# Reordering the attention steps of three engines around four weight products per head

## The chip, the cores and the metric

The kernel runs on one core of a Trainium2 chip. The metric is the device time of one execution in microseconds (us), the median of several runs. Five engines of the core work side by side, each through its own list of instructions in order: TensorE (PE in the profile: matrix products and transposes into the PSUM banks), VectorE (DVE), ScalarE (ACT), GpSimd (POOL, here mainly the issuer of small transfers) and SyncE (SP, which issues the weight transfers). They wait for each other through counting semaphores.

## What is computed

The reference runs two transformer blocks over 256 tokens of width 2048. The first has two layers (neighbourhood, dilated and memory attention); the second has a state-space mixer, differential attention and a gated feed-forward part. The change lies in the differential attention of the second block. Cut to that:

```python
q = rms_norm_2(q, q_norm_w) * 64 ** -0.5        # 8 heads, each with two maps of width 64
k = rms_norm_2(k, k_norm_w)
s = einsum('bqhmd,bkhmd->bhmqk', q, k) + bias   # masked by chunks of 64
p = softmax(s)
p = p[:, :, 0] - lam * p[:, :, 1]
o = einsum('bhqk,bkhe->bqhe', p, v)
o = rms_norm_2(o, subln_w) * (1 - lambda_init)
```

with `q`, `k`, `v` and the state-space input `u` of each head from `h @ w_in`.

## The kernel before

Activations are kept feature-major: 128 features on the partitions, 256 tokens along the row. The weights stream through a ring of four slots of 128x1024 (`w_raw`). Each fp32 chunk is split into two parts: ACT rounds it into `w_hi` (`split_hi`, L717), DVE subtracts into `w_lo` (`split_lo`, L1297), and SP refills the slot when DVE is done with it. PE multiplies each chunk by three products of 8 tiles (L1991 to L1993). Two chunks, 48 products, make one job: 128 output features for all tokens. `split_hi(p, c)` may write a slot only when PE has used up the chunk four places earlier (`w_free`).

The eight heads take one period each, `head_2(i)`, with four jobs (q, k, v, u). While head i is projected, head i-1 goes through scores and softmax (`prev`), and head i-2 through the product with v and the output norm (`prev2`). So every engine carries three heads' steps, written by hand between the jobs:

- PE: job 0, `values2` (probabilities by v), job 1, `scores2` (two transposes and eight score products), `output_sums` (the sum of squares for the output norm, L2180), jobs 2 and 3, `turn2` (transposes of the probabilities, L2203), `norm_sums` (L2211).
- DVE: `split_lo(p, 1)`, u out of PSUM, `attn_0` (q and k norm), `split_lo(p, 2)`, `attn_1` (clamp and square of the output, L1591 and L1593), q out of PSUM, `split_lo(p, 3)`, `attn_2` (bias added and row maxima, L1599 to L1603; mean, `osq` and reciprocal for the output norm, L1607 to L1611), k out of PSUM, `attn_3` (the two softmax maps combined, L1618 to L1627), `split_lo(p, 4)`, v out of PSUM, `attn_4` (output norm applied, L1635 and L1637).
- ACT: `attn_0` (L949, L952), `split_hi(p, 1)`, `attn_1` (Ln, Exp for the q and k norm, L957 and L959; output out of PSUM), `split_hi(p, 2)`, `split_hi(p, 3)`, `attn_2` (v out of PSUM, L976; four Exp, L982; Sqrt, L987), `split_hi(p, 4)`, `attn_3` (squares of q and k, L992).

The third chunk pair of a period is chunks 4 and 5; `split_lo(p, 4)` and `split_hi(p, 4)` already prepare chunks 0 and 1 of the period after. Head 1 has no `prev2` part. The last heads' steps run in the first two of the eight periods of gate products that follow, `gates(p, j, attn=...)`, where the state-space mixer's sections and a Sigmoid per job (`gate_out`, L1029) lie between the same steps. A function of ACT from another table than the last one gets an ACT_TABLE_LOAD ahead of it; the compiler puts it there. Small tensors of this part all lie in one buffer, so the profile names them `arena` or `cols`.

The semaphores that matter: `osq_clamped` (L1593 done) lets PE start `output_sums`; `osum_done` lets DVE start L1607; `ov_step` (L1611 done) lets ACT take the Sqrt; `scores2_done`, `max2_ready` and `exp2_done` lead from the scores over the maxima to the Exps and on to L1618; `probs2_ready` (L1627 done) lets PE start `turn2`.

Of the kernel before, what the change touches and what calls it, by code (L numbers as in the profile page):

```python
# [10 lines left out]
ALU = mybir.AluOpType  # L11
ACT = mybir.ActivationFunctionType
AX_X = mybir.AxisListType.X

P = 128
# [35 lines left out]
SUBLN_EPS = 1e-5  # L51
# [13 lines left out]
FLT_MAX = 3.4028234e38  # L65
SUB_SCALE = 2.0 ** -12
# [3 lines left out]
def build(nc, ap, out):  # L70
    ctx = ExitStack()
    with ctx:
# [253 lines left out]
        osum_done = sem("osum_done")  # L326
# [369 lines left out]
        def _(act):  # L696
# [273 lines left out]
                act.dma_start(u_d[i - 1], zz).then_inc(u_stored, 16)  # L970

            def attn_2(i, prev, prev2):
                if prev:

                    act.wait_ge(scores2_done, i)
                    act.activation(v2_tok, v_ps[:, 0, :].rearrange("p (a b) -> p a b", a=NQ),  # L976
                                   ACT.Copy).then_inc(v2_ready, 1)
                    act.wait_ge(max2_ready, i)
                    for m in range(2):
                        for t in range(NQ):  # L980
                            k = NQ * m + t
                            e = act.activation(sc[m][:, t, :], sc[m][:, t, :], ACT.Exp, bias=neg_max2[:, k:k + 1],  # L982
                                               accum_out=row_sum2[:, k:k + 1])
                    e.then_inc(exp2_done, 1)
                if prev2:
                    act.wait_ge(ov_step, 2 * (i - 1))
                    act.activation(o_root, ov, ACT.Sqrt).then_inc(o_root_ready, 1)  # L987

            def attn_3(p, i):

# [200 lines left out]
        def _(dve):  # L1191
# [401 lines left out]
                    dve.tensor_tensor(osq, osq, osq, ALU.mult).then_inc(osq_clamped, 1)  # L1593

            def attn_2(i, prev, prev2):
                if prev:
                    dve.wait_ge(scores2_done, i)
                    dve.wait_ge(bias2_in, 64 * i)
                    dve.tensor_tensor(sc[0], s_ps[:], bias2, ALU.add)  # L1599
                    dve.tensor_tensor(sc[1], o_ps[:], bias2, ALU.add).then_inc(biased2, 1)  # L1600
                    dve.wait_ge(biased2, i)
                    dve.tensor_reduce(neg_max2[:, 0:2], sc[0], AX_X, ALU.max, negate=True)
                    dve.tensor_reduce(neg_max2[:, 2:4], sc[1], AX_X, ALU.max, negate=True).then_inc(max2_ready, 1)  # L1603
                if prev2:
                    dve.wait_ge(osum_done, i - 1)

                    dve.tensor_scalar(osq, p_ps[:, 0, :], FLT_MAX * SUB_SCALE ** 2, SUB_SCALE, ALU.is_lt, ALU.mult)  # L1607
                    dve.tensor_scalar(ov, p_ps[:, 0, :], 1.0 / P, SUBLN_EPS * SUB_SCALE ** 2,
                                      ALU.mult, ALU.add).then_inc(ov_step, 1)
                    dve.wait_ge(ov_step, 2 * (i - 2) + 1)  # L1610
                    dve.reciprocal(ov, ov).then_inc(ov_step, 1)  # L1611

            def attn_3(i, prev):
                if prev:

                    h = i - 1
                    dve.wait_ge(exp2_done, i)
                    dve.reciprocal(coef2, row_sum2).then_inc(comb_step, 1)  # L1618
                    dve.wait_ge(comb_step, 3 * h + 1)
                    dve.tensor_scalar(coef2[:, 2:4], coef2[:, 2:4], neg_lam, None, ALU.mult).then_inc(comb_step, 1)  # L1620
                    dve.wait_ge(comb_step, 3 * h + 2)
                    for t in range(NQ):
                        e = dve.tensor_scalar(sc[0][:, t, :], sc[0][:, t, :], coef2[:, t:t + 1], None, ALU.mult)
                    e.then_inc(comb_step, 1)
                    dve.wait_ge(comb_step, 3 * h + 3)
                    for t in range(NQ):
                        e = dve.scalar_tensor_tensor(out=sc[0][:, t, :], in0=sc[1][:, t, :],  # L1627
                                                     scalar=coef2[:, 2 + t:3 + t], in1=sc[0][:, t, :],
                                                     op0=ALU.mult, op1=ALU.add)
                    e.then_inc(probs2_ready, 1)  # L1630

            def attn_4(i, prev2):
                if prev2:
                    dve.wait_ge(o_root_ready, i - 1)
                    dve.tensor_tensor(o_root, o_root, osq, ALU.mult).then_inc(om_step, 1)  # L1635
                    dve.wait_ge(om_step, i - 1)
                    dve.scalar_tensor_tensor(out=ov, in0=o_sb, scalar=vecs[:, 2:3], in1=o_root,  # L1637
                                             op0=ALU.mult, op1=ALU.mult).then_inc(yo_ready, 1)

            def head_2(i, prev=True, prev2=True, prev3=True):  # L1640
                p = P_QKV + i
                split_lo(p, 1)
                if prev:
                    if prev2:
                        dve.wait_ge(u_stored, 16 * (i - 1))
                    evac_u(p - 1)
                    dve.wait_ge(z_free, taken(p - 1, 3))
                    dve.sem_inc(u_ready, 1)
                attn_0(i, prev, prev3)
                split_lo(p, 2)  # L1650
                attn_1(i, prev, prev2)
                evac2(qk[:, 0, :], p, 0, 4)
                split_lo(p, 3)
                attn_2(i, prev, prev2)
                evac2(qk[:, 1, :], p, 1, 4)
                attn_3(i, prev)
                split_lo(p, 4)
                if prev:
                    dve.wait_ge(scores2_done, i)
                evac2(v2_t, p, 2, 4)  # L1660
                attn_4(i, prev2)

# [121 lines left out]
            def gates(p, j, first=False, attn=None):  # L1786
                split_lo(p, 1)
                if not first:
                    evac_gate(p - 1, 3, 4 * j - 1)
                if attn is not None:  # L1790
                    attn_0(attn[0], attn[1], attn[3])
                section(4 * j)
                split_lo(p, 2)
                evac_gate(p, 0, 4 * j, first)
                if attn is not None:
                    attn_1(*attn[:3])
                section(4 * j + 1)
                split_lo(p, 3)
                evac_gate(p, 1, 4 * j + 1)
                if attn is not None:  # L1800
                    attn_2(*attn[:3])
                section(4 * j + 2)
                split_lo(p, 4)
                evac_gate(p, 2, 4 * j + 2)
                if attn is not None:
                    attn_3(*attn[:2])
                    attn_4(attn[0], attn[2])
                section(4 * j + 3)


# [168 lines left out]
        def _(pe):  # L1979
# [234 lines left out]
            def head_2(i, prev=True, prev2=True, sums=False):  # L2214
                p = P_QKV + i
                job2(p, 0, x_hi, x_lo, (lambda kt: pe.wait_ge(x_lo_ready, DEPTH * KT + kt + 1)) if sums else None, 4)
                if sums:
                    pe.wait_ge(sq_summed, summed(DEPTH, 0) - 1)
                    pe.matmul(p_ps[:, 0, :], ones[:], sq_sum[:, 0, :], start=True, stop=True)
                    column_sums(p_ps[:, 1, :], sq_sum[:, 1, :], sums_ready)  # L2220
                if prev2:
                    values2(i)
                job2(p, 1, x_hi, x_lo, ring=4)
                if prev:
                    scores2(i, prev2)
                if prev2:
                    output_sums(i)
                job2(p, 2, x_hi, x_lo, ring=4)
                job2(p, 3, x_hi, x_lo, ring=4)
                pe.wait_ge(qk_sq_ready, i + 1)  # L2230
                if prev:
                    turn2(i, prev2)
                norm_sums(i)
# [37 lines left out]
            def gates(p, j, first=False, attn=None):  # L2271
                for c in range(4):
                    job2(p, c, x_hi, x_lo)
                    if attn is not None:
                        i, prev = attn
                        if c == 0:
                            values2(i)
                        if c == 1:
                            if prev:
                                scores2(i, True)  # L2280
                            output_sums(i)
                        if c == 3 and prev:
                            turn2(i, True)
                    for n in range(PAIRS):
                        if FRONT[n] == 4 * j + c:
                            inputs(n)
                        if FRONT[n] + 2 == 4 * j + c:
                            outputs(n)
# [249 lines left out]
```

## Time and profile before

| | |
|---|---|
| median of three runs | 2573.4 us (2573.39 to 2573.99) |
| the profiled execution | 2573.4 us, span 2571.7 us |
| PE busy | 2473.0 us, 96% of the span |
| DVE busy | 1695.0 us, 66% |
| ACT busy | 1214.3 us, 47% |
| POOL busy | 629.8 us, 24% |
| chain that ended last | PE 74%, DVE 12%, issue 5%, ACT 4%, POOL 3% |
| HBM traffic | 189 GB/s over the span |

The time is what the host's runs report; the span is that of the profiled execution's instructions, and 1.7 us lie around it. Matmuls are pipelined: a row of 0.28 us starts every 0.12 us at full clock, so PE's progress is read from start to start and not from the busy column. PE is busy nearly throughout; what is left are waits of one engine for another inside the stages. The eight head periods lie from 1136 to 1358 us, and the two gate periods that still carry attention steps from 1358 to about 1426 us.

### The profile page before, as it was taken

The page shows a single profiled execution, that of the slowest core. Times are in us where ns is not written, and L with a number is a line of the kernel's source. Part 1 is how long each engine was busy: PE and PEld are TensorE (multiplying, and loading weights), DVE is VectorE, ACT ScalarE, POOL GpSimd, SP SyncE. Part 2 cuts the span into 40 slices and gives each one's busy share as a digit, 9 for nine tenths or more (in the row PEclk, how much of TensorE's full clock was granted, in tenths as well). Part 3 has the DMA queues.
Part 4 walks back from the last instruction along what each step waited for, and adds up shares of the span by engine and source line. Part 5 has one row for each costly group of instructions (what it writes and reads, how often), then busy time and mean ns, then how long its engine had stood idle before and what let it go on. Part 6 is the DMA issues. An engine that isn't in the chain of part 4 may idle for free.

```text
span 2571.7 us, 50514 instructions
## 1 busy us (share of the span) xinstructions
PE 2473.0 (96%) x18072; PEld 2348.5 (91%) x18072; DVE 1695.0 (66%) x2556; ACT 1214.3 (47%) x1813; POOL 629.8 (24%) x1047
## 2 busy tenths in 40 slices
PE   7899999989999999999998999999999999999999
PEld 7899999889899999899998999999888888888888
DVE  7877676557777777668887776665555555555555
ACT  5345444445555555555655334434544444444443
POOL 3300031248778887120010231001000000000000
PEclk9999999999999999999999999999999999999999
DMA  6655576555555555456465676665766777667664
GB/s 234 196 189 189 182 212 195 173 174 169 169 178 180 183 192 186 153 164 207 160 194 163 214 253 229 197 218 168 194 191 187 186 189 187 188 185 185 186 187 156
DMA packets 217449, 484.85 MB, mean 189 GB/s; under 512 B 22760, under 2 KB 120724, under 8 KB 217088
## 3 DMA queue, kind: packets, MB, share of 16 engines
q1 hardware_dynamic: 182912, 415.29, 53.2%
q0 software_dynamic: 13216, 37.93, 4.9%
q10 hardware_dynamic: 21216, 30.22, 3.6%
q8 instruction: 67, 1.10, 0.2%
q14 instruction: 38, 0.31, 0.0%
HBM read 455.00 MB, written 31.08 MB: 189 GB/s over the span
## 4 chain that ended last, share of the span: by engine, by line
PE 74%; DVE 12%; issue 5%; ACT 4%; POOL 3%; ACTq 1%; DMA 1%; DVEq 0%; POOLq 0%; SPq 0%
PE z_ps L1991 14%; PE z_ps L1992 13%; PE z_ps L1993 13%; PE z_ps L2328 6%; PE z_ps L2327 6%; PE z_ps L2333 6%; DVE w_lo L1297 4%; ACT w_hi L717 2%; POOL arena L559 1%; PE v_ps L2361 1%; PE o_ps L2362 1%; PE o_ps L2361 1%; PE p_ps L2361 1%; PE p_ps L2360 1%; PE o_ps L2360 1%
## 5 line engine op out<-in xcount | busy, mean ns | idle before, releaser
L1297 DVE TENSOR_TENSOR w_lo<-w_raw,w_hi 128x1024 fp32r<-128x1024 f32 x520 | 638.5, 1256 | 316.3 <-ACT w_hi L717 313.7
L1991 PE MATMUL z_ps<-x_hi,w_hi 128*128 128x256 f32 x2816 | 823.8, 293 | 17.3 <-DVE w_lo L1290 14.2
L1992 PE MATMUL z_ps<-x_lo,w_hi 128*128 128x256 f32 x2816 | 806.9, 287 | 0.0
L1993 PE MATMUL z_ps<-x_hi,w_lo 128*128 128x256 f32 x2816 | 806.5, 286 | 0.0
L717 ACT ACTIVATE w_hi<-w_raw 128x1024 fp32r<-128x1024 f32 x520 | 532.8, 1051 | 264.4 <-PE z_ps L1993 213.4
L1991 PEld LDWEIGHTS z_ps<-x_hi,w_hi 128*128 128x128 f32 x2816 | 550.1, 195 | 24.3 <-issue 16.5
L1992 PEld LDWEIGHTS z_ps<-x_lo,w_hi 128*128 128x128 f32 x2816 | 550.3, 195 | 1.2
L1993 PEld LDWEIGHTS z_ps<-x_hi,w_lo 128*128 128x128 f32 x2816 | 550.1, 195 | 0.0
L1881 DVE TENSOR_TENSOR w_lo<-w_raw,w_hi 128x1024 fp32r<-128x1024 f32 x262 | 320.8, 1226 | 314.8 <-ACT w_hi L1141 314.8
L1141 ACT ACTIVATE w_hi<-w_raw 128x1024 fp32r<-128x1024 f32 x262 | 277.7, 1060 | 427.9 <-PE z_ps L2333 272.8
L2327 PE MATMUL z_ps<-w_hi,x_hi 128*128 128x512 f32 x704 | 275.2, 391 | 0.6 <-DVE res L1857 0.6
L2328 PE MATMUL z_ps<-w_hi,x_lo 128*128 128x512 f32 x704 | 274.4, 390 | 0.0
L1991 PE MATMUL z_ps<-y_hi,w_hi 128*128 128x256 f32 x768 | 220.7, 287 | 14.2 <-DVE y_lo L1344 10.6
L1992 PE MATMUL z_ps<-y_lo,w_hi 128*128 128x256 f32 x768 | 219.0, 285 | 0.0
L1993 PE MATMUL z_ps<-y_hi,w_lo 128*128 128x256 f32 x768 | 218.9, 285 | 0.0
L2333 PE MATMUL z_ps<-w_lo,x_hi 128*128 128x512 f32 x704 | 188.3, 389 | 0.0
L1991 PE MATMUL z_ps<-m_hi,w_hi 128*128 128x256 f32 x576 | 166.6, 289 | 3.9 <-DVE m_lo L1853 2.6
L1991 PEld LDWEIGHTS z_ps<-y_hi,w_hi 128*128 128x128 f32 x768 | 149.0, 194 | 22.0 <-issue 21.9
L1992 PE MATMUL z_ps<-m_lo,w_hi 128*128 128x256 f32 x576 | 163.6, 284 | 0.0
L1993 PE MATMUL z_ps<-m_hi,w_lo 128*128 128x256 f32 x576 | 163.6, 284 | 0.0
L2327 PEld LDWEIGHTS z_ps<-w_hi,x_hi 128*128 128x128 f32 x704 | 132.3, 188 | 27.6 <-DVE res L1857 0.8
L2333 PEld LDWEIGHTS z_ps<-w_lo,x_hi 128*128 128x128 f32 x704 | 132.2, 188 | 27.5
(382 smaller groups left out, 4123.2 us busy)
## 6 DMA issues: line engine op xcount, KB each, us to landing
w_raw<-in_w SPq DMA_DIRECT2D x704, 512.0 KB, 4.2
w_raw<-in_w SPq DMA_DIRECT2D x80, 384.0 KB, 4.9
res<-tab_d POOLq DMA_DIRECT2D x32, 384.0 KB, 4.6
w_raw<-in_w SPq DMA_DIRECT2D x80, 128.0 KB, 2.9
tab_d<-arena ACTq DMA_DIRECT2D x32, 256.0 KB, 2.1
tab_d<-arena POOLq DMA_DIRECT2D x32, 128.0 KB, 3.5
sg_d<-arena ACTq DMA_DIRECT2D x32, 128.0 KB, 4.4
arena<-sg_d POOLq DMA_DIRECT2D x16, 256.0 KB, 3.7
```

The lines of the kernel that those rows point to most:

```text
L717: act.activation(w_hi[:, n % RING, :], w_raw[:, n % RING, :], ACT.Copy).then_inc(w_hi_ready, 1)
L1141: act.activation(w_hi[:, k % RING, :], w_raw[:, k % RING, :], ACT.Copy).then_inc(w_hi_ready, 1)
L1297: dve.tensor_tensor(w_lo[:, n % RING, :], w_raw[:, n % RING, :], w_hi[:, n % RING, :].bitcast(F32), ALU.subtract).then_inc(w_lo_ready, 1)
L1881: dve.tensor_tensor(w_lo[:, k % RING, :], w_raw[:, k % RING, :], w_hi[:, k % RING, :].bitcast(F32), ALU.subtract).then_inc(w_lo_ready, 1)
L1991: pe.matmul(z, wh, hi[:, kt, :], start=(first and i == 0), stop=False)
L1992: pe.matmul(z, wh, lo[:, kt, :], start=False, stop=False)
L1993: m = pe.matmul(z, wl, hi[:, kt, :], start=False, stop=(last and i == len(kts) - 1))
L2327: pe.matmul(z[t], x_hi[:, kt, r], hi_w[:, :, i * P:(i + 1) * P], start=(kt == 0), stop=False)
L2328: pe.matmul(z[t], x_lo[:, kt, r], hi_w[:, :, i * P:(i + 1) * P], start=False, stop=False)
L2333: m = pe.matmul(z[t], x_hi[:, kt, t * P:(t + 1) * P], lo_w[:, :, i * P:(i + 1) * P], start=False, stop=(kt == KT - 1))
L2360: pe.matmul(z, wh, y_hi[:, at + kt, :], start=(kt == 0), stop=False)
L2361: pe.matmul(z, wh, y_lo[:, at + kt, :], start=False, stop=False)
```

## The change

The order of the same instructions is changed on three engines; none is added or dropped in the source.

- PE: `output_sums(i)` now comes ahead of `scores2(i)`, in the heads and in the gate periods.
- DVE: in `attn_2` the output-norm part (L1607 to L1611, with its wait for `osum_done`) comes ahead of bias and maxima. In the head periods the combination of the maps (`attn_3`) moves from ahead of `split_lo(p, 4)` to behind it and behind v's way out of PSUM; `attn_4` is joined to it. In the gate periods `attn_3` and `attn_4` keep their place.
- ACT: in `attn_2` the Sqrt, with its wait for `ov_step`, comes ahead of v's copy and the four Exps.

```diff
--- before.py
+++ after.py
@@ -970,6 +970,9 @@
                 act.dma_start(u_d[i - 1], zz).then_inc(u_stored, 16)
 
             def attn_2(i, prev, prev2):
+                if prev2:
+                    act.wait_ge(ov_step, 2 * (i - 1))
+                    act.activation(o_root, ov, ACT.Sqrt).then_inc(o_root_ready, 1)
                 if prev:
 
                     act.wait_ge(scores2_done, i)
@@ -982,9 +985,6 @@
                             e = act.activation(sc[m][:, t, :], sc[m][:, t, :], ACT.Exp, bias=neg_max2[:, k:k + 1],
                                                accum_out=row_sum2[:, k:k + 1])
                     e.then_inc(exp2_done, 1)
-                if prev2:
-                    act.wait_ge(ov_step, 2 * (i - 1))
-                    act.activation(o_root, ov, ACT.Sqrt).then_inc(o_root_ready, 1)
 
             def attn_3(p, i):
 
@@ -1593,6 +1593,14 @@
                     dve.tensor_tensor(osq, osq, osq, ALU.mult).then_inc(osq_clamped, 1)
 
             def attn_2(i, prev, prev2):
+                if prev2:
+                    dve.wait_ge(osum_done, i - 1)
+
+                    dve.tensor_scalar(osq, p_ps[:, 0, :], FLT_MAX * SUB_SCALE ** 2, SUB_SCALE, ALU.is_lt, ALU.mult)
+                    dve.tensor_scalar(ov, p_ps[:, 0, :], 1.0 / P, SUBLN_EPS * SUB_SCALE ** 2,
+                                      ALU.mult, ALU.add).then_inc(ov_step, 1)
+                    dve.wait_ge(ov_step, 2 * (i - 2) + 1)
+                    dve.reciprocal(ov, ov).then_inc(ov_step, 1)
                 if prev:
                     dve.wait_ge(scores2_done, i)
                     dve.wait_ge(bias2_in, 64 * i)
@@ -1601,16 +1609,8 @@
                     dve.wait_ge(biased2, i)
                     dve.tensor_reduce(neg_max2[:, 0:2], sc[0], AX_X, ALU.max, negate=True)
                     dve.tensor_reduce(neg_max2[:, 2:4], sc[1], AX_X, ALU.max, negate=True).then_inc(max2_ready, 1)
-                if prev2:
-                    dve.wait_ge(osum_done, i - 1)
-
-                    dve.tensor_scalar(osq, p_ps[:, 0, :], FLT_MAX * SUB_SCALE ** 2, SUB_SCALE, ALU.is_lt, ALU.mult)
-                    dve.tensor_scalar(ov, p_ps[:, 0, :], 1.0 / P, SUBLN_EPS * SUB_SCALE ** 2,
-                                      ALU.mult, ALU.add).then_inc(ov_step, 1)
-                    dve.wait_ge(ov_step, 2 * (i - 2) + 1)
-                    dve.reciprocal(ov, ov).then_inc(ov_step, 1)
-
-            def attn_3(i, prev):
+
+            def attn_3(i, prev, prev2):
                 if prev:
 
                     h = i - 1
@@ -1628,8 +1628,6 @@
                                                      scalar=coef2[:, 2 + t:3 + t], in1=sc[0][:, t, :],
                                                      op0=ALU.mult, op1=ALU.add)
                     e.then_inc(probs2_ready, 1)
-
-            def attn_4(i, prev2):
                 if prev2:
                     dve.wait_ge(o_root_ready, i - 1)
                     dve.tensor_tensor(o_root, o_root, osq, ALU.mult).then_inc(om_step, 1)
@@ -1653,12 +1651,11 @@
                 split_lo(p, 3)
                 attn_2(i, prev, prev2)
                 evac2(qk[:, 1, :], p, 1, 4)
-                attn_3(i, prev)
                 split_lo(p, 4)
                 if prev:
                     dve.wait_ge(scores2_done, i)
                 evac2(v2_t, p, 2, 4)
-                attn_4(i, prev2)
+                attn_3(i, prev, prev2)
 
 
 
@@ -1803,8 +1800,7 @@
                 split_lo(p, 4)
                 evac_gate(p, 2, 4 * j + 2)
                 if attn is not None:
-                    attn_3(*attn[:2])
-                    attn_4(attn[0], attn[2])
+                    attn_3(*attn[:3])
                 section(4 * j + 3)
 
 
@@ -2221,10 +2217,10 @@
                 if prev2:
                     values2(i)
                 job2(p, 1, x_hi, x_lo, ring=4)
+                if prev2:
+                    output_sums(i)
                 if prev:
                     scores2(i, prev2)
-                if prev2:
-                    output_sums(i)
                 job2(p, 2, x_hi, x_lo, ring=4)
                 job2(p, 3, x_hi, x_lo, ring=4)
                 pe.wait_ge(qk_sq_ready, i + 1)
@@ -2276,9 +2272,9 @@
                         if c == 0:
                             values2(i)
                         if c == 1:
+                            output_sums(i)
                             if prev:
                                 scores2(i, True)
-                            output_sums(i)
                         if c == 3 and prev:
                             turn2(i, True)
                     for n in range(PAIRS):
```

## Rows read from the trace of the kernel before

**Rows 1.** Windows, one period each: stretch, us, busy (count) PE, PEld, DVE, ACT, POOL, clock, DMA.

```profile
1163.06:1189.29 26.23, 26.23 (x217) 24.94 (x215) 21.34 (x36) 12.83 (x21) 2.39 (x5) 1.00 0.58 185
...
1189.29:1219.40 30.11, 27.68 (x222) 26.05 (x220) 24.61 (x41) 17.83 (x28) 2.09 (x4) 1.00 0.66 225
...
1302.88:1330.61 27.73, 27.52 (x223) 26.06 (x221) 22.96 (x36) 17.78 (x29) 7.60 (x15) 1.00 0.66 213
...
1358.33:1395.18 36.85, 30.17 (x243) 29.12 (x241) 26.42 (x50) 22.23 (x33) 1.10 (x2) 0.95 0.52 165
```

**Rows 2.** Timeline of PE in one head period: start, duration, engine, line, [idle before <-releaser].

```profile
1315.35 0.38 PE L2190 MATMUL v_ps<-ident,arena 128*128 128x128 f32 x2
...
1317.01 0.70 PE L2180 MATMUL p_ps<-arena,ones 128*128 128x256 f32 x2 [0.21 <-DVE arena L1593]
...
1329.07 0.60 PE L2203 MATMUL p_ps<-ident,arena 128*128 128x128 f32 x4
```

**Rows 3.** Timeline of DVE from one head's maxima to the next head's.

```profile
1291.76 0.69 DVE L1599 TENSOR_TENSOR arena<-s_ps,arena 128x512 f32<-128x512 f32 x1
...
1294.27 0.42 DVE L1607 TENSOR_SCALAR arena<-p_ps 128x256 f32<-128x256 f32 x1
...
1296.72 0.36 DVE L1553 TENSOR_TENSOR arena<-z_ps,rstd 128x256 f32<-128x256 f32 x1
...
1297.00 0.17 DVE L1618 RECIPROCAL cols<-cols 128x4 f32<-128x4 f32 x1
...
1299.18 2.36 DVE L1297 TENSOR_TENSOR w_lo<-w_raw,w_hi 128x1024 fp32r<-128x1024 f32 x2 [0.18 <-ACT w_hi L717]
...
1301.79 0.42 DVE L1635 TENSOR_TENSOR arena<-arena 128x256 f32<-128x256 f32 x1
...
1316.54 0.42 DVE L1593 TENSOR_TENSOR arena<-arena 128x256 f32<-128x256 f32 x1
...
1319.48 0.69 DVE L1599 TENSOR_TENSOR arena<-s_ps,arena 128x512 f32<-128x512 f32 x1
```

**Rows 4.** Timeline of ACT over the same stretch.

```profile
1294.39 0.51 ACT L982 ACTIVATE arena<-arena,cols 128x256 f32<-128x256 f32 x1 [4.89 <-DVE cols L1603]
...
1296.49 1.28 ACT L987 ACT_TABLE_LOAD   x1
...
1298.11 1.99 ACT L717 ACTIVATE w_hi<-w_raw 128x1024 fp32r<-128x1024 f32 x2
...
1303.19 1.99 ACT L717 ACTIVATE w_hi<-w_raw 128x1024 fp32r<-128x1024 f32 x2
...
1305.20 1.28 ACT L957 ACT_TABLE_LOAD   x1
...
1308.15 0.63 ACT L957 ACTIVATE arena<-arena 128x512 f32<-128x512 f32 x1 [1.66 <-DVE arena L1567]
```

**Rows 5.** Timeline, head periods 1 and 2: ACT, DVE, PE.

```profile
1184.16 2.00 ACT L717 ACTIVATE w_hi<-w_raw 128x1024 fp32r<-128x1024 f32 x2
...
1188.83 2.46 DVE L1695 SCALAR_TENSOR_TENSOR res<-res,final_g,arena 128x256 f32<-128x256 f32 x6
...
1205.82 0.70 PE L2180 MATMUL p_ps<-arena,ones 128*128 128x256 f32 x2 [1.37 <-DVE arena L1593]
```

**Rows 6.** Timeline, first gate period: ACT, DVE, DVE, PE.

```profile
1386.24 1.28 ACT L1029 ACT_TABLE_LOAD   x1
...
1392.35 0.18 DVE L1618 RECIPROCAL cols<-cols 128x4 f32<-128x4 f32 x1
...
1394.27 0.42 DVE L1635 TENSOR_TENSOR arena<-arena 128x256 f32<-128x256 f32 x1
...
1394.41 1.11 PE L2203 MATMUL p_ps<-ident,arena 128*128 128x128 f32 x4 [6.33 <-DVE arena L1627]
```

**Rows 7.** Timeline of PE behind a wait in the third gate period.

```profile
1441.63 1.08 PE L2252 MATMUL s_ps<-arena,res 128*128 128x64 f32 x8 [1.77 <-issue]
...
1443.13 0.41 PE L1991 MATMUL z_ps<-x_hi,w_hi 128*128 128x256 f32 x1
```

## The prediction

> **What bounds the kernel now.** I read the page first: PE is busy nearly throughout, so a wait of PE anywhere is lost time unless another engine's lag swallows it. Then the windows, one per head period [rows 1]. The change touches only heads 1 to 7 and the first two gate periods. A steady head period takes 27.73 us, and heads 3 to 7 together take 1358.33 - 1219.40 = 138.93 us. Then PE's timeline of one steady period, counted from its first product (1302.88 = zero) [rows 2]: the scores start at +12.47, the output sums at +14.13 after a wait of only 0.21, `turn2` at +26.19, the next period at +27.73. So PE runs almost without a gap, and 27.73 - 0.21 = 27.5 us is its floor; little can be won there. But the 0.21 names a second chain that is only just in time: PE waits for L1593, and DVE starts that at +13.66 [rows 3]. This chain of DVE and ACT has no more than 0.2 us of slack per head, and each step added to it will show. The timelines of DVE and ACT [rows 3, 4] give the step lengths.
>
> **The change part by part.** Nothing is added; what counts is who comes later.
>
> PE: the sums now stand ahead of the scores. PE is free at +12.47, but L1593 is where it was, so PE would wait until about +14.1. Before, the scores, 1.45 us long (1317.01 - 1315.35 - 0.21 [rows 2]), filled that time. Behind the wait are queued the scores and jobs 2 and 3. If S is the start of the sums, PE can reach `turn2` at the earliest at S + 12.06 + 1.45 = S + 13.51 [rows 2].
>
> DVE, `attn_2`: the output-norm part takes 1296.72 - 1294.27 = 2.45 us [rows 3] and now comes ahead of the maxima. L1599 shows no idle time before it [rows 3], so DVE arrives there after the scores; no idle time takes the 2.45 us in, and all of it delays the maxima. Its own wait, for the sums, is met: S is at about +14, DVE there at +16.6 (1319.48 - 1302.88). POOL's transfer of the next head's bias is released by the bias addition, so 2.45 later, and has a period's time.
>
> ACT: Sqrt with its table load (1298.11 - 1296.49 = 1.62 us [rows 4]) moves from behind the Exps into the 4.89 us that ACT spends waiting for the maxima [rows 4]. The wait for `ov_step` stands ahead of v's copy and the Exps, and `split_hi(p, 4)` is queued behind them. The Exps now need a load of their own, since Sqrt has taken the table. The Ln load was issued at 1305.20 while its input came only at 1308.15 [rows 4]: loads run ahead of the wait. The reciprocal is done 2.51 us before the maxima (L1599 to L1607 [rows 3]); Sqrt and copy take some 0.7 (two starts apart as the Exps' four in 2.10 [rows 4], rounded up), the load 1.28, together 2.0, so I cost the new load at nothing, with 0.5 us of cover. Without the cover it costs 1.28 per head. A row shows 1.28 for a load [rows 4]. The Trainium skill, "ScalarE: Activation LUTs", section "What ACT_TABLE_LOAD costs", counts about 2.66 us per switch, a drain included, and the next section says to batch calls by set, which speaks against this order; by 2.66 the load would end 0.9 us after the maxima, about 5 us in all.
>
> DVE, `attn_3`: it moves behind `split_lo(p, 4)` and v. Its wait for the Exps was met on arrival (L1618 shows no idle time [rows 3]), so the move saves no wait. Now `turn2` is late instead. The chain from S to `turn2`: L1593 starts 0.47 before S (1317.01 - 1316.54); to `attn_2` 2.94 (1319.48 - 1316.54); output norm 2.45; maxima 2.51; to the Exps 0.12 (1294.39 - 1294.27); Exps 2.10 (1296.49 - 1294.39); `split_hi` to `split_lo` 1.07 (1299.18 - 1298.11); `split_lo(p, 4)` and v 2.61 (1301.79 - 1299.18); L1618 to `turn2` 2.06 (1394.41 - 1392.35) [rows 2, 3, 4, 6]. Sum: 15.86 - 0.47 = 15.39 us, against PE's 13.51. PE waits 1.88 us at `turn2` in every head.
>
> S itself: in the new order L1635 comes 0.14 before `turn2` (1394.27, 1394.41 [rows 6]), and `turn2` is 1.54 before the next period (1330.61 - 1329.07 [rows 1, 2]), so DVE stands at -1.68 where it stood at -1.09 (1301.79 [rows 3]): 0.59 earlier. ACT's copy of the turned probabilities doesn't get earlier, and ACT's next `split_hi` started at +0.31 [rows 4]. The gain lies between 0 and 0.59; I take 0.4. S = 14.13 - 0.39 = 13.74, `turn2` at 29.13, period 30.67: 2.94 us more than 27.73.
>
> Sum over the heads:
> - Head 1 has no output norm. ACT's `split_hi` is where it was, 1184.16 [rows 5]; + 1.07 + 2.61 + 2.06 + 1.54 = 1191.44 against 1189.29: + 2.15.
> - Head 2: its DVE work starts behind six updates of `res` (L1695), at 1188.83 before; now L1618 at 1187.84 and 1.92 to the place of L1635 (1394.27 - 1392.35), so 0.93 later. S = 1205.82 + 0.93 = 1206.75 [rows 5]; + 15.39 + 1.54 = 1223.68 against 1219.40: 4.28 so far.
> - Heads 3 to 7: 5 x 30.67 = 153.35 against 138.93: + 14.42, so 18.70.
> - First gate period: `turn2` already waits 6.33 us there [rows 6]. Maxima 2.45 later, Sqrt and load off the way to the Sigmoid and `split_hi` (- 1.62 from a head; its load at 1386.24 stays), start 0.5 earlier as above: + 0.3. PE's products for the mixer that wait for the bias addition come up to 2.45 later too, but they lie ahead of that wait and shorten it. The second gate period has no scores: nothing.
>
> Together + 19.0. The profiled execution took 2573.4 us (span 2571.7, 1.7 around it), the same as the median, so 2592.4, rounded 2592. Nothing behind the attention takes it back: PE is the bound there, and the ring of four weight slots holds no lead to spend.
>
> The bounds of what the trace doesn't show. S without the 0.4: + 2. The new load: 0 to 1.28 per head. PE's clock: a wait of 1.77 us in the gate periods was followed by a product of 0.41 us [rows 7], at the lower of the two levels, 1.2 GHz; head 2, with a wait of 1.37 [rows 5], kept a granted clock of 1.00 [rows 1]. The waits of 1.88 at `turn2` lie near the first. What a drop costs I bound by the first gate period, whose granted clock is 0.95 over 36.85 us [rows 1]: 0.05 x 36.85 = 1.8 us of products lost at most. It would fall on job 0, ahead of the wait at the sums (13.74 - 12.47 = 1.27), which takes most of it. Price: 0 to 0.5 per head, 3.7 in all; I take none.
>
> **The rivals.**
> - Only the sums wait; the combined maps come in time. It needs them 1.9 us earlier than my sum. Heads 3 to 7: 5 x (13.74 + 13.51 + 1.54) = 143.95, + 5.0; head 2 + 1.5; gate + 0.3: 2580. For it: the sum has nine terms. Against: each is a row.
> - The Exps' load lies open, issued only when the maxima are there: 1.28 x 7 = 9.0 more, 2601. Against: the Ln load ran ahead [rows 4]. The skill's page on ScalarE tables named above would put it in between, at 2597.
> - The clock stays down so long that the sums' wait does not take it: 7 x 1.8 = 12.6 more, 2605. Against: the wait of 1.27 stands right behind the slow job.
> - The other side: no loss. DVE would have to reach `attn_2` before the scores, so that the output norm ran in idle time; it decides at 2.45 us of idle time before L1599, where the rows show none. Then heads run at 27.5 (6 x 0.2 less) and the gate period saves 1.62: 2570.6, no real change. That the new order changes nothing anywhere belongs here too.
>
> **How the numbers follow.** Forecast 0.76, only the sums 0.08, open load 0.05, clock 0.04, no loss 0.07. The forecast's own range is 2588 to 2596 (S late, + 2; part of the clock's 3.7; below, each head's sum off by some 0.6, 4 in all). The stated range, 2580 to 2597, takes in the sums-only case and leaves out the other three, under 2 in 10. 0.2% is 5.1 us, about what a measurement tells from no change. Slower by over that: all but the last case, 0.92 after a little for surprises; within: 0.05; faster: 0.03.
>
> **What would show it.** A steady head period near 30.7 us. PE idle ahead of L2180 about 1.3 us per head and ahead of `turn2` about 1.9, released by DVE's combination. An ACT_TABLE_LOAD ahead of the Exps that ends before the maxima. DVE idle some 3 us ahead of `split_lo(p, 4)`, waiting for ACT. `turn2`'s wait in the first gate period shorter than 6.33, at nearly the same place counted from that period's start. The prediction is wrong if the head period stays under 29 us, or if time turns up outside 1163 to 1396 us.

## The result and the profile after

The changed kernel takes 2591.56 us (median of four runs, 2587.49 to 2593.14) against 2573.39 (2571.91 to 2573.99): ratio 1.0069, 95% interval 1.0051 to 1.0087. That is 18.2 us slower; 19.0 was forecast. Its profiled execution took 2586.4 us with a span of 2584.7, some 5 us less than its median, so the loss is read period by period and not from the two spans.

The windows of the kernel after, cut at the first product of each period as in [rows 1]; the columns are the same:

```profile
1159.54:1189.32 29.78, 27.69 (x217) 25.46 (x215) 23.33 (x40) 13.03 (x22) 2.38 (x5) 0.95 0.59 191
1189.32:1220.23 30.91, 28.20 (x222) 26.36 (x220) 22.62 (x35) 19.31 (x31) 2.09 (x4) 0.99 0.62 214
...
1281.96:1312.69 30.73, 27.90 (x222) 26.06 (x221) 22.96 (x36) 18.84 (x30) 2.09 (x4) 1.00 0.46 146
1374.12:1410.74 36.62, 30.38 (x242) 29.13 (x241) 25.93 (x48) 22.23 (x33) 1.10 (x2) 0.97 0.43 142
...
1159.54:1374.12 214.58, 195.39 (x1536) 182.12 (x1534) 161.34 (x257) 125.64 (x194) 21.54 (x41) 0.99 0.52 171
1410.74:1742.66 331.92, 318.06 (x2604) 316.44 (x2603) 224.94 (x407) 135.36 (x186) 61.50 (x107) 0.98 0.68 223
```

and two such stretches of the kernel before:

```profile
1163.06:1358.33 195.27, 191.46 (x1537) 181.26 (x1535) 160.91 (x256) 118.91 (x188) 21.50 (x41) 1.00 0.56 184
1395.18:1729.89 334.71, 319.63 (x2604) 317.97 (x2603) 224.97 (x407) 135.51 (x186) 61.49 (x107) 0.97 0.68 221
```

A steady head takes 30.73 us instead of 27.73 [rows 1]. Heads 1 to 7 together take 214.58 instead of 195.27, + 19.31. DVE's work in them is the same to half a microsecond (161.34 and 160.91): nearly all the added time is waiting. ACT counts six instructions more (194 and 188), the added table loads of heads 2 to 7. PE's 3.9 us more of busy time are in part head 1's products at the lower clock (0.95). The first gate period is 0.23 us shorter. The two spans differ by only 13.0 us because other stretches were shorter in this execution: head 1 begins 3.5 us earlier, and the stretch behind the gate period is 2.8 us shorter. The first is no part of the change. Two waits of PE in the first block's early heads, which both kernels run alike, were 4.71 and 3.73 us before and 2.33 and 2.75 after. For the 2.8 us I have no cause.

PE's timeline in the steady period that begins at 1281.96; the counterpart is [rows 2]:

```profile
1295.70 0.70 PE L2176 MATMUL p_ps<-arena,ones 128*128 128x256 f32 x2 [1.12 <-DVE arena L1593]
1296.23 0.38 PE L2186 MATMUL v_ps<-ident,arena 128*128 128x128 f32 x2
...
1311.10 0.65 PE L2199 MATMUL p_ps<-ident,arena 128*128 128x128 f32 x4 [1.71 <-DVE arena L1627]
```

Counted from the period's start (1281.96), the sums begin at +13.74 and `turn2` at +29.14. PE waits 1.12 us for the square and 1.71 us for the combined maps. Before it waited only at the sums, for 0.21. DVE in the same period (counterpart [rows 3]):

```profile
1295.21 0.43 DVE L1593 TENSOR_TENSOR arena<-arena 128x256 f32<-128x256 f32 x1
...
1298.16 0.42 DVE L1599 TENSOR_SCALAR arena<-p_ps 128x256 f32<-128x256 f32 x1
...
1300.61 0.63 DVE L1607 TENSOR_TENSOR arena<-s_ps,arena 128x512 f32<-128x512 f32 x1
...
1303.07 0.41 DVE L1553 TENSOR_TENSOR arena<-z_ps,rstd 128x256 f32<-128x256 f32 x1
1306.25 2.36 DVE L1297 TENSOR_TENSOR w_lo<-w_raw,w_hi 128x1024 fp32r<-128x1024 f32 x2 [2.77 <-ACT w_hi L717]
1308.53 0.42 DVE L1553 TENSOR_TENSOR arena<-z_ps,rstd 128x256 f32<-128x256 f32 x1
1308.86 0.17 DVE L1618 RECIPROCAL cols<-cols 128x4 f32<-128x4 f32 x1
```

The output norm (L1599 here) now runs from 1298.16 to 1300.61, and the maxima follow. DVE then stands idle for 2.77 us ahead of `split_lo(p, 4)`, with the combination queued behind it. ACT (counterpart [rows 4]):

```profile
1295.69 1.28 ACT L975 ACT_TABLE_LOAD   x1
1300.73 0.42 ACT L975 ACTIVATE arena<-arena 128x256 f32<-128x256 f32 x1 [3.76 <-DVE arena L1603]
1301.05 0.37 ACT L979 ACTIVATE arena<-v_ps 128x256 f32<-128x256 f32 x1
1301.44 1.28 ACT L985 ACT_TABLE_LOAD   x1
1303.18 0.51 ACT L985 ACTIVATE arena<-arena,cols 128x256 f32<-128x256 f32 x1 [0.46 <-DVE cols L1611]
...
1305.17 1.99 ACT L717 ACTIVATE w_hi<-w_raw 128x1024 fp32r<-128x1024 f32 x2
...
1311.79 0.60 ACT L949 ACTIVATE arena<-p_ps 128x512 f32<-128x512 f32 x1 [4.11 <-PE p_ps L2199]
```

Both loads run while ACT would wait anyway. The added one ends at 1302.72, and ACT still waits 0.46 us for the maxima. The Exp begins 1.74 us after the load began. Where nothing but the load is waited for, the function follows after 1.29 us (the Sqrt in after_old_act below, 1279.41 to 1280.70). By the 2.66 us that the Trainium skill gives for a switch ("ScalarE: Activation LUTs", "What ACT_TABLE_LOAD costs"), the Exp would have begun at 1304.1 at the earliest, an estimate from that page; the trace does not agree with it here.

### The profile page after: what moved, and what is told of

It is laid out like the page before. It is cut to its first block, busy times and chain, and to the rows that moved or that the text cites. A ratio compares the mean times of both kernels' runs of the same rounds, so it can differ in the third digit from the quotient of the medians.

```text
span 2584.7 us, 50520 instructions
## 1 busy us (share of the span) xinstructions
PE 2476.3 (96%) x18072; PEld 2348.0 (91%) x18072; DVE 1691.9 (65%) x2556; ACT 1220.9 (47%) x1819; POOL 628.6 (24%) x1047
## 4 chain that ended last, share of the span: by engine, by line
PE 69%; DVE 15%; issue 7%; ACT 5%; POOL 2%; ACTq 1%; DVEq 0%; DMA 0%; POOLq 0%
PE z_ps L1987 12%; PE z_ps L1988 12%; PE z_ps L1989 12%; PE z_ps L2323 6%; PE z_ps L2324 6%; PE z_ps L2329 6%; DVE w_lo L1297 5%; ACT w_hi L717 2%; PE o_ps L2358 1%; PE o_ps L2357 1%; PE o_ps L2356 1%; PE v_ps L2357 1%; PE v_ps L2356 1%; PE p_ps L2357 1%; PE v_ps L2358 1%
```

## The experiments

Two theories could both explain 18 us. **One loop**: DVE, ACT and PE hand each period round, and a step costs time only where it lies on the longest way round. **Own waits**: each move costs the wait that PE shows for it, and the waits add. Five runs undo or make one move at a time (the order of the output norm on DVE was neither made nor undone alone), and two more take the loop theory to the gate periods. "Section" is from the first product of head 1 to `turn2` of the first gate period, 231.35 us before; it leaves out what differs elsewhere. The first column is the usual period of heads 3 to 7, or their range where it is wider than 0.3 us. All ratios are to the kernel before, measured on the same chip.

| kernel | steady head | section | median | ratio, 95% interval |
|---|---|---|---|---|
| before | 27.73 | 231.35 | 2572.95 | |
| after | 30.73 | 250.44 | 2591.56 | 1.0069, 1.0051 to 1.0087 |
| only_combine | 29.2 to 31.7 | 246.68 | 2585.16 | 1.0045, 1.0026 to 1.0064 |
| after_old_combine | 28.8 to 30.9 | 244.44 | 2583.45 | 1.0040, 1.0023 to 1.0057 |
| only_pe | 28.81 | 239.48 | 2579.45 | 1.0018, 1.0005 to 1.0031 |
| after_old_pe | 30.75 | 250.49 | 2588.98 | 1.0056, 1.0038 to 1.0075 |
| after_old_act | 32.3 to 34.0 | 267.03 | 2609.04 | 1.0140, 1.0119 to 1.0161 |

The median of before was 2573.39 beside after, 2572.96 beside after_old_act and 2572.95 beside the other four.

**only_combine**: of the three moves, only that of the combination.

```diff
                 evac2(qk[:, 1, :], p, 1, 4)
-                attn_3(i, prev)
                 split_lo(p, 4)
                 if prev:
                     dve.wait_ge(scores2_done, i)
                 evac2(v2_t, p, 2, 4)
+                attn_3(i, prev)
                 attn_4(i, prev2)
```

> The kernel before with one of the three moves: in the head periods the combination of the two maps stands behind the second half's low split and v's way out. Theory of one loop (DVE, ACT and PE hand the period round, and a step counts only if it lies on the longest way round): Sqrt and its load still lie between the Exps and ACT's next weight split, so a steady head period of 12.47 + ... = 29.8 us (2.94 + 2.51 + 0.12 + 2.10 + 1.62 + 1.07 + 2.61 + 2.06 - 0.47 = 14.56 from the sums to turn2, sums at 13.74, 1.54 behind), against 27.7 before and 30.7 after; about 2587 us. Theory of own waits (each move costs the wait that PE shows for it, and they add): PE's wait at turn2 of 1.7 us alone, 7 times, 29.4 a head, about 2585. This run can't tell the two apart well; it says how much of the loss the one move carries.

Measured: 2585.16 us. The head periods swing between 29.18 and 31.67 around the expected 29.8. The longest goes with a lower clock of PE. Two waits at `turn2`:

```profile
1247.73 1.11 PE L2203 MATMUL p_ps<-ident,arena 128*128 128x128 f32 x4 [2.53 <-DVE arena L1627]
...
1278.26 0.65 PE L2203 MATMUL p_ps<-ident,arena 128*128 128x128 f32 x4 [1.46 <-DVE arena L1627]
```

Behind 2.53 us the same transposes take 1.11 us, the lower level, and behind 1.46 they take 0.65. The window that ends with the first of them, 31.67 us long, has a granted clock of 0.95. Alone, this move lengthens the section by 15.3 us, where all of the changes together make 19.1. What the lower clock takes is in the 15.3. The median lies by the number of own waits (2585), 2 us under the loop's; as expected, this run does not decide.

**after_old_combine**: the changed kernel without that move.

```diff
                 evac2(qk[:, 1, :], p, 1, 4)
+                attn_3(i, prev)
                 split_lo(p, 4)
                 if prev:
                     dve.wait_ge(scores2_done, i)
                 evac2(v2_t, p, 2, 4)
-                attn_3(i, prev, prev2)
+                attn_4(i, prev2)
```

> The changed kernel with the combination put back ahead of the low split in the heads; sums first on PE and output norm first on DVE and ACT stay. One loop: the output norm no longer runs while ACT does the Exps, so DVE stands still for the Exps (2.1 us) on its own way round; DVE's loop is 29.5 us a head, about 2584. Own waits: only the wait at the sums stays, 27.5 + 1.3 = 28.8 a head, about 2580.

Measured: 29.37 and 29.39 us in heads 4 and 5, 2583.45 us. That is the loop's number, 0.6 above own waits. Heads 6 and 7 are not steady:

```profile
1309.03:1339.90 30.87, 29.21 (x223) 27.27 (x221) 22.97 (x36) 19.25 (x31) 8.20 (x16) 0.94 0.58 193
1339.90:1368.70 28.80, 27.69 (x223) 26.05 (x221) 22.96 (x37) 17.95 (x27) 2.54 (x5) 1.00 0.52 169
```

In head 6 PE's clock fell behind the sums, some 1.5 us were lost (30.87 - 29.38), and in head 7, whose start this had put off, the sums began at +13.73 instead of +14.31 and the period took own waits' 28.8. That DVE and ACT had caught up fits the loop, but no run shows it by itself. Head 2 took 33.86 us, as in only_pe below. So the median, near the loop's 2584, may hold some 4 us of lower clock (1.5, and 2.3 in head 2, estimates from this one trace) and does not decide; heads 4 and 5 do, and DVE's timeline shows where the difference sits:

```profile
1301.32 0.42 DVE L1553 TENSOR_TENSOR arena<-z_ps,rstd 128x256 f32<-128x256 f32 x1
1303.56 0.18 DVE L1618 RECIPROCAL cols<-cols 128x4 f32<-128x4 f32 x1 [1.82 <-ACT arena L985]
```

With the output norm ahead of the maxima, nothing is left for DVE to do during the Exps, and it stands still for 1.82 us. In the order before, L1618 came without a wait [rows 3]: there the 2.45 us of the output norm filled that time.

**only_pe**: the kernel before with PE's swap alone.

```diff
-                if prev:
-                    scores2(i, prev2)
                 if prev2:
                     output_sums(i)
+                if prev:
+                    scores2(i, prev2)
```

(and the same swap in the gate periods)

> The kernel before with the sums ahead of the scores on PE, nothing else. Both theories: PE waits about 1.6 us for the square and does the scores after it: sums at 13.74 to 13.82, 13.51 to turn2, 1.54 to the next period, 28.8 to 28.9 us a head, PE's wait at the sums 1.3 us; about 2580.

Measured: 28.81 us a head and 2579.45 us, as both had it (heads 4 to 7); PE waits 1.12 us at the sums. Head 2 is an exception with 33.91 us, where some 31.6 were to be had (30.11 before, and 1.5):

```profile
1186.50:1220.41 33.91, 30.02 (x222) 27.58 (x221) 24.69 (x41) 18.13 (x30) 2.09 (x4) 0.90 0.62 218
```

```profile
1203.02 1.22 PE L2180 MATMUL p_ps<-arena,ones 128*128 128x256 f32 x2 [3.89 <-DVE arena L1593]
```

PE waits 3.89 us there and the granted clock falls to 0.90; the product that takes 0.70 us elsewhere takes 1.22.

**after_old_pe**: the changed kernel with PE's swap taken back (the diff above, read from + to -).

> The changed kernel with PE's order put back: scores first, then sums. One loop: the scores have 0.7 us and more to spare before DVE takes them, turn2 waits for DVE anyway, so the head period stays at 30.7 us and the time at that of the changed kernel, 2590 to 2592; the wait at turn2 grows from 1.7 to about 3. Own waits: the 1.1 to 1.4 us at the sums are won back in each of six heads, 29.5 a head, about 2584.

Measured: 30.75 us a head, the section 250.49 us against 250.44. Own waits had the head at 29.5. That theory falls here.

```profile
1311.60 0.65 PE L2199 MATMUL p_ps<-ident,arena 128*128 128x128 f32 x4 [3.12 <-DVE arena L1627]
```

The wait at the sums is gone and the one at `turn2` has grown from 1.71 to 3.12. The 1.1 us was moved, not won. Alone, the same swap costs 1.1 us per head (only_pe); in company it costs nothing.

**after_old_act**: the changed kernel with the Sqrt behind the Exps again.

```diff
             def attn_2(i, prev, prev2):
-                if prev2:
-                    act.wait_ge(ov_step, 2 * (i - 1))
-                    act.activation(o_root, ov, ACT.Sqrt).then_inc(o_root_ready, 1)
                 if prev:
...
                     e.then_inc(exp2_done, 1)
+                if prev2:
+                    act.wait_ge(ov_step, 2 * (i - 1))
+                    act.activation(o_root, ov, ACT.Sqrt).then_inc(o_root_ready, 1)
```

> The changed kernel with ACT's order put back: Exps first, Sqrt and its table load behind them. One loop: 1.62 us more between the Exps and ACT's weight split in six heads, 32.3 us a head, about 2602. Own waits: PE never waits for the Sqrt and a table load is saved per head, so 30.7 a head or less, 2590 to 2592.

Measured: 2609.04 us, 17.5 more than after; 33.2 to 34.0 us in heads 3 to 6, 32.31 in head 7. The direction is the loop's, own waits had no loss, and the size is 7 us beyond the loop's number. Lines of PE, ACT and DVE:

```profile
1286.95 1.11 PE L2199 MATMUL p_ps<-ident,arena 128*128 128x128 f32 x4 [3.53 <-DVE arena L1627]
1287.99 1.97 PE L2207 MATMUL s_ps<-arena,ones 64*64 64x256 f32 x8
1289.90 0.58 PE L1987 MATMUL z_ps<-x_hi,w_hi 128*128 128x256 f32 x1
```

```profile
1279.41 1.28 ACT L987 ACT_TABLE_LOAD   x1
1280.70 0.42 ACT L987 ACTIVATE arena<-arena 128x256 f32<-128x256 f32 x1
1281.03 1.99 ACT L717 ACTIVATE w_hi<-w_raw 128x1024 fp32r<-128x1024 f32 x2
...
1288.10 0.60 ACT L949 ACTIVATE arena<-p_ps 128x512 f32<-128x512 f32 x1 [4.57 <-PE p_ps L2199]
```

```profile
1268.70 0.43 DVE L1593 TENSOR_TENSOR arena<-arena 128x256 f32<-128x256 f32 x1
...
1271.14 1.23 DVE L1297 TENSOR_TENSOR w_lo<-w_raw,w_hi 128x1024 fp32r<-128x1024 f32 x1 [0.55 <-ACT w_hi L717]
1272.28 0.42 DVE L1599 TENSOR_SCALAR arena<-p_ps 128x256 f32<-128x256 f32 x1
...
1284.71 0.17 DVE L1618 RECIPROCAL cols<-cols 128x4 f32<-128x4 f32 x1
```

Load and Sqrt delay ACT's split by 1281.03 - 1279.41 = 1.62 us, as expected. The wait at `turn2` of 3.53 us is followed by the lower clock: from `turn2` to the next period are 2.95 us instead of 1.54. Expected 32.3 plus this 1.41 is 33.7, close to the 33.57 of this head (1256.33 to 1289.90), but the loop does not run over PE's 1.41. Against the steady head of after, three pieces are longer. From L1599 to L1618 on DVE it is 12.43 us instead of 10.70, + 1.73: load and Sqrt. ACT's copy of the slower transposes (L949) starts 1.15 us behind `turn2` instead of 0.69, + 0.46. From L1593 to L1599 it is 3.58 us instead of 2.95, + 0.63: DVE waits 0.55 for a weight split that ACT could take up only when PE, slow in job 0, had used up the slot. Together 2.82 of the 2.84 us (33.57 - 30.73); some 1.7 are the order and 1.1 the clock. Of the three orders changed, ACT's is the one that helps, given the other two.

**gate_combine** and **gate_combine_split**: the loop theory also says where the old order loses. In the first gate period the maps are combined behind the low split, DVE stands idle with the Exps done, and PE waits 6.33 us [rows 6]. So the kernel before, with the move the other way:

```diff
                 section(4 * j + 2)
+                if attn is not None:
+                    attn_3(*attn[:2])
                 split_lo(p, 4)
                 evac_gate(p, 2, 4 * j + 2)
                 if attn is not None:
-                    attn_3(*attn[:2])
                     attn_4(attn[0], attn[2])
```

> The kernel before with one move the other way, in the gate periods alone: the combination of the maps stands ahead of DVE's low split of the next period's first chunks. DVE stood idle there 4.7 us with the Exps done, so the maps are combined at about 1387 instead of 1394 and PE's wait of 6.33 us at turn2 goes. In its place PE waits for the weights, whose high split ACT starts only at 1388.4: the next product at about 1390.8 instead of 1395.2. One loop: 4.4 us less, with the clock's drop spared up to 5.8; 2568 to 2569. Own waits: 6.3 less, 2567.

and, in the second, ACT as well:

```diff
                 split_hi(p, 3)
+                ahead = attn is not None and attn[1]
+                if ahead:
+                    split_hi(p, 4)
                 if attn is not None:
                     attn_2(*attn[:3])
                 gate_out(4 * j + 1)
                 section(4 * j + 2)
-                split_hi(p, 4)
+                if not ahead:
+                    split_hi(p, 4)
```

> As the run before, and ACT's split of the next period's first chunks stands ahead of v's copy and the Exps in the first gate period: PE has used up the chunk in that slot at about 1380, and ACT idles until 1382.4. Then neither the maps nor the weights are late: PE goes on at 1388.5 instead of 1395.2, and its clock stays up. 6.7 us less, with the clock 8: 2565 to 2567. If the split delays the Exps (it ends at 1382 at the earliest), up to 1 us of that is lost.

Measured: gate_combine 2566.81 us against 2572.96, ratio 0.9982 (0.9968 to 0.9995). gate_combine_split 2565.27 us, ratio 0.9979 (0.9967 to 0.9992). PE behind job 3 of that period, first the one, then the other:

```profile
1390.39 0.60 PE L2204 MATMUL p_ps<-ident,arena 128*128 128x128 f32 x4
1394.80 0.58 PE L1992 MATMUL z_ps<-x_hi,w_hi 128*128 128x256 f32 x1 [3.81 <-DVEq L1749]
```

```profile
1387.39 0.60 PE L2208 MATMUL p_ps<-ident,arena 128*128 128x128 f32 x4
1388.99 0.39 PE L1996 MATMUL z_ps<-x_hi,w_hi 128*128 128x256 f32 x1 [1.00 <-DVEq L1753]
```

The wait at `turn2` is gone in both. In the first, a wait of 3.81 us stands in its place. Its releaser is not the weights, as I had expected, but the semaphore behind gate output 2: the gate periods use two PSUM banks, the next period's job 0 needs the bank of job 2, and DVE empties it behind `split_lo(p, 4)`, which itself waits 2.83 us for ACT's late high split. From the period's start to the next product are 1394.80 - 1360.79 = 34.0 us instead of 36.85, so 2.8 won and not 4.4. With ACT's split early it is 1388.99 - 1357.77 = 31.2, so 5.6 won and not 6.7, and the clock stays up (0.39 for the product, not 0.56 to 0.58). The clock also bears on the second gate period, here up to the output sums in it; before, then the one, then the other:

```profile
1395.18:1411.26 16.08, 16.08 (x123) 15.98 (x122) 11.43 (x29) 7.52 (x12) 3.25 (x6) 0.90 0.56 175
```

```profile
1394.80:1412.11 17.31, 17.31 (x121) 17.21 (x122) 12.30 (x30) 7.87 (x13) 3.27 (x6) 0.83 0.68 222
```

```profile
1388.99:1403.70 14.71, 14.71 (x120) 14.61 (x121) 11.69 (x27) 6.31 (x10) 3.27 (x6) 1.00 0.66 229
```

Counted to that point, gate_combine has 1.6 us left of its gain, and gate_combine_split has 7.0 (6.7, with the clock 8, expected). The medians moved by 6.2 and 7.7. The intervals of the ratios reach from 1.3 to 8.2 us and from 2.1 to 8.5, so these traces do not contradict the medians, and what gate_combine gained beyond 1.6 is not traced to a cause. gate_combine_split has the lowest median of all kernels here; the intervals of the two overlap.

## Why the prediction was right

**The sum.** Forecast 2592.4, measured 2591.56. Step by step in the steady head: sums at 13.74, measured 13.74; `turn2` at 29.13, measured 29.14; period 30.67, measured 30.73. The wait at `turn2` is 1.71 instead of 1.88, since PE's way with the sums first is a little longer than 13.51. Two terms of the chain were off and cancel, which is luck: the Exps took 1.99 us (1303.18 to 1305.17), not 2.10, and L1618 to `turn2` 2.24 (1308.86 to 1311.10), not the 2.06 that I had taken from the gate period. The 0.4 us by which I let the loop start earlier was my choice between 0 and 0.59, so its exact hit is luck too. The rows show what gives it, before and after:

```profile
1302.87 0.42 ACT L952 ACTIVATE y_hi<-arena 128x256 f32 x1 [0.29 <-DVE arena L1637]
```

```profile
1281.55 0.41 ACT L952 ACTIVATE y_hi<-arena 128x256 f32 x1
1281.85 2.00 ACT L717 ACTIVATE w_hi<-w_raw 128x1024 fp32r<-128x1024 f32 x2
```

DVE now ends the output norm earlier, ACT no longer waits 0.29 us for it, and ACT's split starts 0.11 us ahead of the period instead of 0.31 behind it [rows 4]. Over heads 1 to 7 the period sum was + 19.31 (18.70 forecast), with the gate period + 19.08.

**Maxima late, nothing hides them.** Right: 2.45 us between 1298.16 and 1300.61 with no idle time ahead. **Combination late.** Right: DVE idle 2.77 us ahead of the low split (some 3 forecast), `turn2` released by L1627. **New table load at nothing.** Right, with 0.46 us of cover (0.5 forecast); so the rival of the open load falls. That the cover matters is only argued: no run took it away. The rival's 7 x 1.28 also counted one load too many: in the first gate period the Exps had a load of their own before, so six are new.

**Only the sums wait.** This rival is what PE's swap does alone: only_pe shows 28.81 us per head where it had 28.79. In the changed kernel it was not the case, and after_old_pe shows that the swap carries none of the loss there.

**Head 1 and the clock.** Here the working was off, though the sum was not. Head 1 grew by 3.55 us, not by 2.15, and head 2 by 0.80, not by 2.13; together 4.35 against 4.28. In head 1, a wait of 2.09 us at `turn2` brought PE to the lower clock:

```profile
1186.48 1.01 PE L2199 MATMUL p_ps<-ident,arena 128*128 128x128 f32 x4 [2.09 <-DVE arena L1627]
1187.42 1.97 PE L2207 MATMUL s_ps<-arena,ones 64*64 64x256 f32 x8
1189.32 0.58 PE L1987 MATMUL z_ps<-x_hi,w_hi 128*128 128x256 f32 x1
```

From `turn2` to the next period are 2.84 us instead of 1.54. I had bounded a drop at 1.8 us and put all of it on job 0, where the wait at the sums takes it. In fact `turn2` and the norm sums, slow as well, come first. In head 2 the chain of DVE and ACT starts at DVE's updates of `res` and does not pass through these slow products: the sums begin 43.70 us behind head 1's start (1203.24 - 1159.54), where 43.69 was forecast (1206.75 - 1163.06), and the 1.3 us was swallowed by the wait at them. Where the loop does pass through PE's slow transposes and job 0, as in after_old_act, some 1.1 us is paid in such a head. The steady heads of the changed kernel kept a clock of 1.00 with waits of 1.71 us at `turn2`, so the clock rival fell. Not by much: in head 6 of after_old_combine the clock fell behind a wait of 1.66 us at the sums, and its heads 4 and 5 kept it with 1.69 and 1.68.

**The gate period.** Forecast + 0.3, measured - 0.23: the wait at `turn2` is 4.61 us instead of 6.33, at 35.86 us of the period instead of 36.08. **Nothing behind takes it back.** The stretch behind was 2.8 us shorter in one execution, while the medians differ by 18.2; by these I call the step right, but one trace of each kernel does not show it.

## What to carry to other kernels

Where three engines hand work round in turn, cost a reordering by walking once round the loop with the start times of the old trace; a step moved off one engine's wait and onto another's is not paid twice, and undoing one move of several may win nothing. Ask what used to fill each wait: the output norm on DVE had filled the time of the Exps, and the combination of the maps that of ACT's weight split. And where an engine stands idle with its next-but-one step ready, as DVE did in the gate period, that is the place to reorder; look first at what else is queued behind the step that is passed, here the emptying of a PSUM bank.

## What the runs showed of the hardware that was not expected

PE's clock does not follow the length of one wait alone. Waits of 3.0 to 3.2 us at `turn2` (after_old_pe, six heads) were followed by transposes of 0.65 us and a next product of 0.38 or 0.39 us, the upper level, and the granted clock of heads 3 to 7 was 1.00; waits of 1.66 (head 6, after_old_combine, at the sums), 2.09 (head 1, after), 2.53 (only_combine) and 3.53 us (after_old_act) were followed by the lower level. What decides between them no run here tells. Once down, the small products behind the wait double too: the eight norm sums took 1.9 us instead of 1.0, and the four transposes 1.0 instead of 0.5 to 0.6, start to start.
